# Woven weight blocks and dense products walked backwards in a two-layer hybrid encoder trunk

## What is computed

```python
def swiglu(x, w_gate, w_up, w_down):
    return (jax.nn.silu(x @ w_gate) * (x @ w_up)) @ w_down
...
for layer in range(DEPTH):
    h = h + 0.5 * swiglu(rmsnorm(h, ...), ff1_w_gate, ff1_w_up, ff1_w_down)
    hn = rmsnorm(h, norm_mix[layer])
    h = h + (conv_ssm_mixer(hn, ...) if layer % 2 == 0 else window_attention(hn, ...))
    h = h + 0.5 * swiglu(rmsnorm(h, ...), ff2_w_gate, ff2_w_up, ff2_w_down)
```

## Time and profile before

| | |
|---|---|
| median of 3 runs | 1912.97 us |
| lowest, highest | 1912.39, 1914.33 us |
| profiled execution, first to last instruction (span) | 1910.1 us |
| TensorE matmul busy | 1895.6 us (99%), 13887 instructions |
| TensorE weight load busy | 1788.7 us (94%), 13887 instructions |
| VectorE busy | 956.5 us (50%) |
| ScalarE busy | 599.5 us (31%) |
| mean granted TensorE clock | 0.999 |

### The profile page before, as it was taken

How to read it: one execution, slowest core, us unless ns; L and a number is a source line. 1 busy time by engine, 2 the same in 40 slices (tenths; PEclk the granted TensorE clock), 3 DMA queues, 4 the chain that set the end, 5 groups by cost and what they waited for, 6 DMA issues and landing times.

```text
span 1910.1 us, 33827 instructions
## 1 busy us (share of the span) xinstructions
PE 1895.6 (99%) x13887; PEld 1788.7 (94%) x13887; DVE 956.5 (50%) x1077; ACT 599.5 (31%) x707; POOL 351.3 (18%) x629
## 2 busy tenths in 40 slices
PE   8999999999999999999999999999999999999999
PEld 8999999999999999999999999999987778888887
DVE  5443356668765443344554433345557654434443
ACT  5222222332243222222342222223456532222232
POOL 2888789314230000000000000000012000000000
PEclk9999999999999999999999999999999999999999
DMA  6322444547523332432243323322321233233322
GB/s 180 89 83 83 140 145 126 160 127 189 125 67 89 89 86 83 117 86 74 69 124 88 83 83 99 89 80 69 111 72 45 67 89 100 81 98 100 104 69 86
DMA packets 330785, 188.29 MB, mean 99 GB/s; under 512 B 8152, under 2 KB 323832, under 8 KB 330712
## 3 DMA queue, kind: packets, MB, share of 16 engines
q1 hardware_dynamic: 323296, 166.81, 31.5%
q0 software_dynamic: 7088, 20.38, 4.1%
q10 hardware_dynamic: 328, 0.07, 0.0%
HBM read 174.91 MB, written 11.14 MB: 97 GB/s over the span
## 4 chain that ended last, share of the span: by engine, by line
PE 96%; DVE 2%; issue 1%; ACT 1%; ACTq 0%; POOL 0%; DVEq 0%
PE ps L793 79%; PE ps L1009 5%; PE ps L1051 2%; PE ps L1120 2%; PE ps L1070 1%; PE ps L1259 1%; PE ps L1221 1%; PE ps L1161 0%; PE ps L970 0%; PE ps L969 0%; PE ps L960 0%; PE ps L838 0%; PE ps L1182 0%; PE ps L853 0%; PE ps L1172 0%
## 5 line engine op out<-in xcount | busy, mean ns | idle before, releaser
L793 PE MATMUL ps<-xl,wh 128*128 128x264 f32 (+1 forms) x2432 | 564.5, 302 | 0.0
L793 PE MATMUL ps<-xh,wh 128*128 128x264 f32 (+1 forms) x2432 | 563.5, 301 | 0.8 <-DVE t_a L1610 0.7
L793 PE MATMUL ps<-xh,wl 128*128 128x264 f32 (+1 forms) x2432 | 563.2, 301 | 0.0
L1557 DVE TENSOR_TENSOR wl<-raw,wh 128x2048 fp32r<-128x2048 f32 x171 | 399.9, 2339 | 172.8 <-ACT wh L1270 172.8
L1270 ACT ACTIVATE wh<-raw 128x2048 fp32r<-128x2048 f32 x172 | 327.7, 1905 | 253.0 <-PE ps L793 211.2
L793 PEld LDWEIGHTS ps<-xh,wh 128*128 128x128 f32 x2432 | 390.4, 188 | 17.7 <-DVE t_a L1610 0.9
L793 PEld LDWEIGHTS ps<-xl,wh 128*128 128x128 f32 x2432 | 389.3, 189 | 15.5 <-issue 0.2
L793 PEld LDWEIGHTS ps<-xh,wl 128*128 128x128 f32 x2432 | 389.0, 189 | 14.8
L793 PE MATMUL ps<-act_h,wh 128*128 128x264 f32 (+1 forms) x1232 | 285.1, 301 | 0.0
L793 PE MATMUL ps<-act_l,wh 128*128 128x264 f32 (+1 forms) x1232 | 285.1, 301 | 0.0
L793 PE MATMUL ps<-act_h,wl 128*128 128x264 f32 (+1 forms) x1232 | 284.7, 301 | 0.0
(11 more groups left out here) (308 smaller groups left out, 1721.0 us busy)
## 6 DMA issues: line engine op xcount, KB each, us to landing
raw<-in_ff_w_gate SPq DMA_DIRECT2D x88, 512.0 KB, 4.0
raw<-in_ff_w_up SPq DMA_DIRECT2D x87, 512.0 KB, 5.2
raw<-in_ff_w_down SPq DMA_DIRECT2D x64, 384.0 KB, 4.1
raw<-in_ff_w_down SPq DMA_DIRECT2D x64, 320.0 KB, 3.7
raw<-in_even_w_in SPq DMA_DIRECT2D x16, 512.0 KB, 5.4
raw<-in_attn_w_qkv SPq DMA_DIRECT2D x12, 512.0 KB, 4.3
raw<-in_even_w_out SPq DMA_DIRECT2D x8, 512.0 KB, 4.6
raw<-in_attn_w_o SPq DMA_DIRECT2D x8, 512.0 KB, 4.7
```

The lines of the kernel that those rows point to most:

```text
L793: last = nc.tensor.matmul(ps[:, 2 * pair + hf, 0:nh], w[:, slot, b * P:(b + 1) * P], x[:, k0 + k, c0 + hf * nh:c0 + (hf + 1) * nh], start= ...
L1557: v.tensor_tensor(wl[:, c % 2, :], raw[:, c % 2, :], wh[:, c % 2, :].bitcast(F32), ALU.subtract).then_inc(wl_ready, 1)
```

## The change

Two helpers describe a woven unit: blocks 2q and 2q+1 share 256 elements, with the columns of the first at the even places and those of the second at the odd ones. `woven` is the view in which the splits write, `in_blocks` the plain view in which they read `raw`, and `block_of` picks a block as 128 columns with a step of two elements. `backwards` turns a view round along its last dimension.

```diff
+        def woven(ap):
+            return ap.rearrange("p (q c t) -> p q t c", t=2, c=P)
+        def in_blocks(ap):
+            return ap.rearrange("p (q t c) -> p q t c", t=2, c=P)
+        def block_of(w, slot, b):
+            return w[:, slot, b // 2 * 2 * P:(b // 2 + 1) * 2 * P].rearrange("p (c t) -> p t c", t=2)[:, b % 2, :]
+        def backwards(ap):
+            return ap[:, ::-1]
...
-                            last = nc.tensor.matmul(ps[:, 2 * pair + hf, 0:nh], w[:, slot, b * P:(b + 1) * P],
-                                                    x[:, k0 + k, c0 + hf * nh:c0 + (hf + 1) * nh],
+                            last = nc.tensor.matmul(backwards(ps[:, 2 * pair + hf, 0:nh]), block_of(w, slot, b),
+                                                    backwards(x[:, k0 + k, c0 + hf * nh:c0 + (hf + 1) * nh]),
...
-                        last = nc.tensor.matmul(ps[0:width, bank, 0:KVW], x[:, k, c0:c0 + width], w[:, slot, k % 4 * KVW:(k % 4 + 1) * KVW],
+                        last = nc.tensor.matmul(in_blocks(ps[0:width, bank, 0:KVW]), x[:, k, c0:c0 + width], woven(w[:, slot, k % 4 * KVW:(k % 4 + 1) * KVW]),
...
-                    block = lambda w, w3: w3[:, b // 4, b % 4 * P:(b % 4 + 1) * P] if d < 6 else w[:, (WO[0] + d // 2) % 2, b * P:(b + 1) * P]
+                    block = lambda w, w3: w3[:, b // 4, b % 4 * P:(b % 4 + 1) * P] if d < 6 else block_of(w, (WO[0] + d // 2) % 2, b)
...
-                nc.scalar.activation(wh[:, c % 2, :], raw[:, c % 2, :], ACT.Copy).then_inc(wh_ready, 1)
+                nc.scalar.activation(woven(wh[:, c % 2, :]), in_blocks(raw[:, c % 2, :]), ACT.Copy).then_inc(wh_ready, 1)
...
-                v.tensor_tensor(wl[:, c % 2, :], raw[:, c % 2, :], wh[:, c % 2, :].bitcast(F32), ALU.subtract).then_inc(wl_ready, 1)
+                v.tensor_tensor(woven(wl[:, c % 2, :]), in_blocks(raw[:, c % 2, :]), woven(wh[:, c % 2, :].bitcast(F32)), ALU.subtract).then_inc(wl_ready, 1)
```

More of the change, by code:

```diff
@@ L837, in first_job @@
                         for hf in range(nb):
-                            last = nc.tensor.matmul(ps[:, hf, 0:nh], w[:, 0, k * P:(k + 1) * P], x[:, k, c0 + hf * nh:c0 + (hf + 1) * nh],
+                            last = nc.tensor.matmul(backwards(ps[:, hf, 0:nh]), block_of(w, 0, k), backwards(x[:, k, c0 + hf * nh:c0 + (hf + 1) * nh]),
                                                     start=(k == 0 and q == 0), stop=(k == KD - 1 and q == 2))
@@ L852, in second_job @@
                         for hf in range(nb):
-                            last = nc.tensor.matmul(ps[:, 2 + hf, 0:nh], w[:, 0, (KD + k) * P:(KD + k + 1) * P], x[:, k, c0 + hf * nh:c0 + (hf + 1) * nh],
+                            last = nc.tensor.matmul(backwards(ps[:, 2 + hf, 0:nh]), block_of(w, 0, KD + k), backwards(x[:, k, c0 + hf * nh:c0 + (hf + 1) * nh]),
                                                     start=(k == 0 and q == 0), stop=(k == KD - 1 and q == 2))
@@ L1008, in _ @@
                         for hf in range(2):
-                            last = nc.tensor.matmul(ps[:, 2 * (p % 2) + hf, 0:L // 2], w[:, slot, b * P:(b + 1) * P], x[:, k, hf * L // 2:(hf + 1) * L // 2],
+                            last = nc.tensor.matmul(backwards(ps[:, 2 * (p % 2) + hf, 0:L // 2]), block_of(w, slot, b), backwards(x[:, k, hf * L // 2:(hf + 1) * L // 2]),
                                                     start=(k == 0 and q == 0), stop=(k == KD - 1 and q == 2))
@@ L1022, in glu_blocks @@
                         for hf in range(2):
-                            last = nc.tensor.matmul(ps[:, 2 * (j % 2) + hf, 0:L // 2], w[:, GLU[0] % 2, b * P:(b + 1) * P], x[:, 2 * KC + k, hf * L // 2:(hf + 1) * L // 2],
+                            last = nc.tensor.matmul(backwards(ps[:, 2 * (j % 2) + hf, 0:L // 2]), block_of(w, GLU[0] % 2, b), backwards(x[:, 2 * KC + k, hf * L // 2:(hf + 1) * L // 2]),
                                                     start=(k == 0 and q == 0), stop=(k == KC - 1 and q == 2))
@@ L1050, in _ @@
                         for hf in range(2):
-                            last = nc.tensor.matmul(ps[:, 2 * (d % 2) + hf, 0:L // 2], w[:, slot, b * P:(b + 1) * P], x[:, k, hf * L // 2:(hf + 1) * L // 2],
+                            last = nc.tensor.matmul(backwards(ps[:, 2 * (d % 2) + hf, 0:L // 2]), block_of(w, slot, b), backwards(x[:, k, hf * L // 2:(hf + 1) * L // 2]),
                                                     start=(k == 0 and q == 0), stop=(k == KD - 1 and q == 2))
@@ L1119, in query_part @@
                     for q, (w, x) in enumerate(((wh, xh), (wh, xl), (wl, xh))):
-                        last = nc.tensor.matmul(ps[:, 2 + t, :], w[:, slot, b * P:(b + 1) * P], x[:, k, c0:c0 + width],
+                        last = nc.tensor.matmul(backwards(ps[:, 2 + t, :]), block_of(w, slot, b), backwards(x[:, k, c0:c0 + width]),
                                                 start=(k == 0 and q == 0), stop=(k == KD - 1 and q == 2))
@@ L1220, in out_part @@
                     for q, (w, x) in enumerate(((wh, act_h), (wh, act_l), (wl, act_h))):
-                        last = nc.tensor.matmul(ps[:, 2 + d, :], w[:, (WO[0] + d // 2) % 2, b * P:(b + 1) * P], x[:, k, c0:c0 + width],
+                        last = nc.tensor.matmul(backwards(ps[:, 2 + d, :]), block_of(w, (WO[0] + d // 2) % 2, b), backwards(x[:, k, c0:c0 + width]),
                                                 start=(k == 0 and q == 0), stop=(k == KD - 1 and q == 2))
@@ L1256, in _ @@
                     b = d % 2 * KD + k
-                    block = lambda w, w3: w3[:, b // 4, b % 4 * P:(b % 4 + 1) * P] if d < 6 else w[:, (WO[0] + d // 2) % 2, b * P:(b + 1) * P]
+                    block = lambda w, w3: w3[:, b // 4, b % 4 * P:(b % 4 + 1) * P] if d < 6 else block_of(w, (WO[0] + d // 2) % 2, b)
                     for q, (w, x) in enumerate(((block(wh, w3h), act_h), (block(wh, w3h), act_l), (block(wl, w3l), act_h))):
-                        last = nc.tensor.matmul(ps[:, d - 4, :], w, x[:, k, c0:c0 + width], start=(k == 0 and q == 0), stop=(k == KD - 1 and q == 2))
+                        last = nc.tensor.matmul(backwards(ps[:, d - 4, :]), w, backwards(x[:, k, c0:c0 + width]), start=(k == 0 and q == 0), stop=(k == KD - 1 and q == 2))
                 last.then_inc(tile_full, 1)
@@ L1359, in _ @@
             act.wait_ge(gate_landed, 16)
-            nc.scalar.activation(wh[:, 0, 0:GW], raw[:, 0, 0:GW], ACT.Copy).then_inc(gate_split[0], 1)
+            nc.scalar.activation(woven(wh[:, 0, 0:GW]), in_blocks(raw[:, 0, 0:GW]), ACT.Copy).then_inc(gate_split[0], 1)
             act.wait_ge(init_evac, NT + 2)
@@ L1366, in _ @@
             act.wait_ge(raw_landed[0], 32)
-            nc.scalar.activation(wh[:, 0, GW:2 * GW], raw[:, 0, GW:2 * GW], ACT.Copy).then_inc(wh_ready, 1)
+            nc.scalar.activation(woven(wh[:, 0, GW:2 * GW]), in_blocks(raw[:, 0, GW:2 * GW]), ACT.Copy).then_inc(wh_ready, 1)
             act.wait_ge(var_ready, 1)
@@ L1510, in half_high @@
                 act.wait_ge(tile_full, j0 + 2 * NKV)
-                nc.scalar.activation(wh[:, c % 2, at], raw[:, c % 2, at], ACT.Copy).then_inc((half_split, wh_ready)[hf], 1)
+                nc.scalar.activation(woven(wh[:, c % 2, at]), in_blocks(raw[:, c % 2, at]), ACT.Copy).then_inc((half_split, wh_ready)[hf], 1)
             for t in range(2):
@@ L1660, in gate_low @@
             def gate_low(at):
-                v.tensor_tensor(wl[:, 0, at], raw[:, 0, at], wh[:, 0, at].bitcast(F32), ALU.subtract).then_inc(gate_split[1], 1)
+                v.tensor_tensor(woven(wl[:, 0, at]), in_blocks(raw[:, 0, at]), woven(wh[:, 0, at].bitcast(F32)), ALU.subtract).then_inc(gate_split[1], 1)
             dve.wait_ge(gate_split[0], 1)
@@ L1994, in quarter_low @@
                     dve.wait_ge(wh_ready, c + 1)
-                low = v.tensor_tensor(wl[:, c % 2, at], raw[:, c % 2, at], wh[:, c % 2, at].bitcast(F32), ALU.subtract)
+                low = v.tensor_tensor(woven(wl[:, c % 2, at]), in_blocks(raw[:, c % 2, at]), woven(wh[:, c % 2, at].bitcast(F32)), ALU.subtract)
                 if q == 3:
```

6 lines of the change are left out of this document (3 added, 3 removed).

## The result

The changed kernel takes 1928.51 us (median, 1927.79 to 1930.44), the kernel before 1912.68 us beside it: ratio 1.0084, 95% interval 1.0071 to 1.0097. It is 15.8 us slower; 1863 us was forecast, 50 us faster. The first rival (1933 us, from 1920 to 1963) is the one that came about. The profiled execution took 1930.44 us and its span is 1928.4 us. The 2.0 us between the two is what lies ahead of the first and behind the last instruction; it is 1.8 to 2.1 us in every execution whose span is recorded, the kernel before included, so the 2.9 us given for it ahead of the prediction compared the span of one execution with the median of others.

What follows compares the result with a forecast made beforehand. TensorE's matmul spacing was taken as the bound, 12.4 or 18.5 ns above the columns because load and moving row meet. Terms -70 + 20 + 0 + 0 = -50 us gave 1863 us, range 1785 to 1945.

Steps and rivals of the forecast that it cites:

- The first rival: Stream stays as it is, key and value products halve in rate: +20 us, up to 50 with splits; 1933 us, chance 0.20.
- Woven weights, moving rows backwards: In the matmul stream, load and moving row at one pace and direction stop meeting: 5.5 ns a matmul, 70 us less.
- The second rival: Load and moving row don't disturb each other and a step of two elements costs nothing: 1913 us, chance 0.10.
- Keys and values: In 96 key and value matmuls, moving weights read at a step of two elements halve the column rate: +20 us.
- Banks: Same columns of the same bank written in the other order: gain taken as 0.
- Splits: Writing `wh` and `wl` and reading `wh` at a step of 8 bytes: taken as 0, up to 30 us in the range.

Runs made afterwards that it cites:

- the walk alone: The changed kernel with moving rows and banks walked backwards but all weights plain, no weaving: 1908.33 us, ratio 0.9979 to the kernel before.
- the version with 264 columns only: The kernel with rows and banks backwards and no weaving, but forwards in products with one row of 512: 1904.1 us, ratio 0.9954 to the kernel before.

## Why the prediction was wrong

**What bounds the kernel.** Right: TensorE's spacing, not waits. Nearly all of the differences above are differences of spacing or of the clock.

**The failed step: "Woven weights, moving rows backwards", -70 us.** It measured 10,752 x -0.91 = -9.8 us with 264 columns and (1920 + 48) x 1.66 = +3.3 us with 512, together -6.5 us. What failed first is the mechanism. The reading behind the term, that load and moving row meet, was put together from the excess and its repeating scatter. Both are real, but the runs take the inference apart: half the load removes 0.9 ns of 12.4, doubling its pace beside rows walked backwards removes nothing at 264 columns and 0.5 ns at 512 beyond what turning the rows does alone, and a row that stands still removes 9.6. The excess goes with the moving row's own walk, and so does the scatter. Evening the scatter out did not lower the mean: of the kernels whose rows of 512 are walked through memory at full width, the changed one has the most even starts, and they come 1.7 ns later than before. The size failed too: the shortest step of a scatter was taken as the price without the disturbance, and read off rounded times. In whole nanoseconds the short end of the spacings before was 225 and 116, 7 and 6 ns under their means and not 11. By the rule of the Trainium skill that the prediction weighed ("TensorE: Matmul & The Clock Gate", Part 2, the LDWEIGHTS step: separate read ports), the load takes nothing from the running matmul; the run with half a load agrees to within 0.9 to 1.2 ns. The 0.5 ns that weaving costs beside rows read forwards is the clearer sign that the two are not wholly independent. The second rival, which rested on that rule, had the mechanism nearly right for the stream (-6.5 us in place of 0), and failed on the keys and values.

**Keys and values, +20 us.** Right: +21.25 us in the chain, +20.3 us by taking it out and +22.3 us by adding it alone. The halved column rate was the right bound. That the earlier trace rows pointed to it is in part luck: they are writes, of other engines and at wider steps, and on these very engines a step of two costs 9 to 13% and 1%.

**Banks, 0.** Right (1911.97 against 1912.07 us). "PSUM — Partial Sum Buffer", Specifications, in the Trainium skill, says that a pattern that isn't contiguous slows matmuls significantly; a bank written from its last column to its first doesn't count as one here, at a ratio of 0.9999 (0.9990 to 1.0009).

**Splits, 0.** Right for the end, not in their own length: ScalarE's grew by 0.25 us against a possible 1.7, VectorE's by 0.02 against 1.8. The cover of the earlier trace rows was still enough. The timeline of VectorE in the changed kernel:

```profile
972.40 0.71 DVE L1609 SCALAR_TENSOR_TENSOR h<-ps,h 128x528 f32 x1 [0.78 <-PE ps L809]
...
976.61 2.29 DVE L1573 TENSOR_TENSOR wl<-raw,wh 128x2048 fp32r<-128x2048 f32 x1 [1.15 <-ACT wh L1286]
```

The split ends 6.5 us after the tile before, with 7.3 us to the next. TensorE waited 0.9 us for a low split, once, behind a slow transfer (10.4 us, at 354 us of the span).

**The sum.** -9.8 + 3.3 + 21.25 + 1.6 (clock) = +16.3 us. The medians differ by 15.8 us, but the profiled executions, from which the terms are read, by 18.3 us (1928.4 against 1910.1). So 2 us are not in the terms, 1.6 of them ahead of the keys and values, where the wait of 0.9 us lies; the nearer agreement with the medians is in part luck. The same terms give -9.8 + 4.3 + 1.6 = -3.9 us for the walk alone (measured -3.9) and -9.8 + 1.6 = -8.2 us for the version with 264 columns only (measured -8.0); in both profiles the eight slow matmuls are there too, and all 16 executions of these two kernels have a mean granted clock of 0.997 or 0.998, while most of the kernel before have 0.999.

**Chances.** The forecast had 0.55 on an inference that no row could test and whose direction was an assumption. The rival that rested on measured rows had 0.20.

**Left open.** Why a row walked backwards is quicker at 264 columns and slower at 384 and 512, and why the starts scatter by the block. No run moved the tiles to other addresses. That the load runs from the last column to the first, as the prediction assumed, no run shows. Why ScalarE's split is longer with weaving and the walk together than with weaving alone isn't known either. In which executions the clock falls, and why a mean of 0.998 or less comes more often with rows walked backwards, is open.

## What to carry to other kernels

Where a matmul takes longer than its columns, let the moving row stand still and halve the load before naming a cause: only the two runs together part the row's own walk from the load. Keep the moving operand at a step of one element in float32; the stationary one can bear a step of two (195 ns in place of 188, 0.5 ns of spacing), not of four beside 264 columns. When a layout change helps one form of product, measure each form apart: here backwards for 264 columns and forwards for 512 took 1904.1 us, backwards for all 1908.3 and forwards for all 1912.1.

## What the runs showed of the hardware

- Both readers of TensorE, the moving row's and the load's, seem to be held to about 9 bytes of address range per ns in a partition, once the 2.7 ns that a standing row leaves over its columns are taken off. Estimates worked out from the runs: the plain row, 1056 bytes in 122.36 - 2.7 ns, 8.8; 2048 bytes in 229.2 ns, 8.9; the row at a step of two, 4096 bytes in 457 - 2.7 ns, 9.0; the load at a step of four, 2048 bytes in 234.1 ns, 8.7. The load at a step of two asks for less (1024 bytes in 121 ns) and is nearly free. This is a pattern in four numbers, not a tested mechanism, and it says nothing of the direction.
- A moving row that reads one column again and again starts every 112.8 ns at 264 columns and 216.0 at 512, and without scatter.
- The direction in which a bank is written makes no difference; that in which a row is read makes -0.7% at 264 columns, +0.3% at 384 and +0.9% at 512.
- With woven units ScalarE's split took 9 to 13% longer and VectorE's 1% or less. The rows with steps of eight and 66 elements in the earlier trace rows took 89% (ScalarE, eight) and 62 to 77% (VectorE) longer than their plain neighbours; some of these also read another buffer.
- Some 1.8 us of two-column products were followed by 3.2 us at a granted clock of 0.50 in some executions and not in others of the same kernel: with the bank alone backwards the profiled execution has the slow matmuls (7.08 us for the 24), 0.997 and 1914.03 us, while seven of its ten executions have 0.999 and 1911.3 to 1912.3 us.
